# Modulation halves in another order and at other places, key and query projections interleaved by halves

## The reference

```python
def adaln_params(cond, w_mod, b_mod):
    m = jax.nn.silu(cond) @ w_mod + b_mod          # w_mod[i]: 1024 x 6144
    return jnp.split(m, N_MOD, axis=-1)            # six components of 1024

# layer 0: attention; layer 1: pooling; then both the same:
hx = modulate(x, sh1, sc1)                         # h * (1 + scale) + shift
x = layer_norm(ALPHA * x + g1 * y_lat, ln_g[i, 0], ln_b[i, 0])
x = layer_norm(ALPHA * x + g2 * swiglu(modulate(x, sh2, sc2), ffn_w_in[i], ffn_w_out[i]),
               ln_g[i, 1], ln_b[i, 1])
```

## Time and profile before

| | us |
|---|---|
| three runs, median (lowest, highest) | 1374.47 (1372.9, 1379.59) |
| the profiled execution, its own time | 1374.82 |
| its span in the trace | 1373.0 |
| TensorE busy | 1189.5 (87%) |
| VectorE busy | 819.4 (60%) |
| ScalarE busy | 489.8 (36%) |
| mean granted clock of TensorE, share of full speed | 0.932 |

### The profile page before, as it was taken

How to read it: one execution, slowest core, us unless ns; L and a number is a source line. 1 busy time by engine, 2 the same in 40 slices (tenths; PEclk the granted TensorE clock), 3 DMA queues, 4 the chain that set the end, 5 groups by cost and what they waited for, 6 DMA issues and landing times.

```text
span 1373.0 us, 17100 instructions
## 1 busy us (share of the span) xinstructions
PE 1189.5 (87%) x7007; PEld 1011.6 (74%) x7007; DVE 819.4 (60%) x1163; ACT 489.8 (36%) x676; POOL 92.3 (7%) x33
## 2 busy tenths in 40 slices
PE   3899997777777897799999699949999898899998
PEld 1676865677666876699997588847877646799977
DVE  3557476476666766776555665677865425555543
ACT  3224334232222232333433344523444433433332
POOL 0000100000000000000000002321224200000000
PEclk9899998989889999899999899978899999999999
DMA  9991531728666668259555346601012244455553
GB/s 347 327 323 62 214 117 51 283 72 288 219 225 230 249 230 291 77 177 303 185 188 176 116 157 214 184 32 62 32 62 92 65 145 137 132 184 178 183 185 111
DMA packets 145663, 236.97 MB, mean 173 GB/s; under 512 B 4918, under 2 KB 86323, under 8 KB 145459
## 3 DMA queue, kind: packets, MB, share of 16 engines
q1 hardware_dynamic: 138656, 221.12, 47.5%
q10 hardware_dynamic: 6930, 14.77, 3.3%
HBM read 229.32 MB, written 6.55 MB: 172 GB/s over the span
## 4 chain that ended last, share of the span: by engine, by line
PE 62%; DVE 13%; issue 9%; DMA 7%; ACT 5%; POOL 2%; SPq 1%; ACTq 1%; POOLq 0%; DVEq 0%
PE bank L525 59%; DMA ring<-in_ffn_w_in 7%; DVE ring_lo L1360 4%; ACT w_hi L1029 3%; DVE modacc L1481 3%; PE bank L567 3%; POOL small L2133 1%; SPq L2188 1%; POOL ring_lo L2124 1%; DVE small L2008 1%; DVE y_tok L1669 1%; DVE small L1672 1%; ACT hc_hi L1078 0%; ACTq L1061 0%; DVE y_tok L1666 0%
## 5 line engine op out<-in xcount | busy, mean ns | idle before, releaser
L1360 DVE TENSOR_TENSOR ring_lo<-ring,w_hi 128x2048 fp32r<-128x2048 f32 (+4 forms) x142 | 314.3, 2214 | 328.6 <-ACT w_hi L1029 328.6
L1029 ACT ACTIVATE w_hi<-ring 128x2048 fp32r<-128x2048 f32 (+4 forms) x154 | 285.8, 1858 | 517.6 <-PE bank L525 410.4
L525 PE MATMUL bank<-h_hi,w_hi 128*128 128x256 f32 x1056 | 303.8, 288 | 3.7 <-DVE h_lo L1379 2.1
L525 PE MATMUL bank<-h_lo,w_hi 128*128 128x256 f32 x1056 | 299.6, 284 | 0.0
L525 PE MATMUL bank<-h_hi,ring_lo 128*128 128x256 f32 x1056 | 299.3, 283 | 0.0
L525 PEld LDWEIGHTS bank<-h_hi,w_hi 128*128 128x128 f32 x1056 | 204.0, 193 | 6.9 <-issue 6.9
L525 PEld LDWEIGHTS bank<-h_lo,w_hi 128*128 128x128 f32 x1056 | 203.7, 193 | 2.3 <-issue 2.3
L525 PEld LDWEIGHTS bank<-h_hi,ring_lo 128*128 128x128 f32 x1056 | 203.5, 193 | 0.0
L525 PE MATMUL bank<-w_hi,h_hi 128*128 128x512 f32 (+4 forms) x320 | 130.5, 408 | 10.1 <-DVE h_lo L1600 4.4
L525 PE MATMUL bank<-ring_lo,h_hi 128*128 128x512 f32 (+4 forms) x320 | 126.4, 395 | 0.0
L525 PE MATMUL bank<-w_hi,h_lo 128*128 128x512 f32 (+4 forms) x320 | 125.9, 393 | 0.0
(11 more groups left out here) (223 smaller groups left out, 1598.8 us busy)
## 6 DMA issues: line engine op xcount, KB each, us to landing
aux<-in_w_mod SPq DMA_DIRECT2D x24, 2048.0 KB, 9.8
ring<-in_ffn_w_in SPq DMA_DIRECT2D x88, 512.0 KB, 5.8
ring<-in_w_in SPq DMA_DIRECT2D x24, 1024.0 KB, 4.9
ring<-in_w_ffn_in SPq DMA_DIRECT2D x44, 512.0 KB, 4.6
ring<-in_ffn_w_out SPq DMA_DIRECT2D x20, 1024.0 KB, 5.2
ring<-in_attn_w_qkv SPq DMA_DIRECT2D x12, 1024.0 KB, 13.1
ring<-in_w_ffn_out SPq DMA_DIRECT2D x10, 1024.0 KB, 5.0
bias_rows<-srow ACTq DMA_DIRECT2D x1, 5376.0 KB
```

Of the source, the lines that this page charges most:

```text
L525: return nc.tensor.matmul(o, l, r, start=start, stop=stop, **kw)
L1029: nc.scalar.activation(panel_part(i, 0), raw_panel(i), ACT.Copy).then_inc(w_hi, 1)
L1360: V.tensor_tensor(panel_part(i, 1), raw_panel(i), panel_part(i, 0).bitcast(F32), ALU.subtract)\
```

## The change

The order of the ten later components becomes 2, 3, 4, 9, 5, 6, 7, 8, 10, 11 (`COMPS`), and their products stand elsewhere: halves 0 to 7 in attention, 8 to 13 in ffn0_in (blocks 0, 2, 3, 5, 6, 8), 14 to 17 in ffn0_out, in quarters, and 18 and 19 in ffn1_in as before. `halves_before` places their loads anew. The first group's keys and queries run as K half 0, Q half 0, K half 1, Q half 1, with the second pair of first loads, the transposes of the later half of the tokens and their products on banks 6 and 7 behind Q half 0. The second group's keys begin behind the first transposed probabilities. On the output projection of attention the last loop runs tokens outside, columns inside, and VectorE makes the low parts of panels 16 and 17 behind the statistics. Both halves of the folded pooling rows are made in block 10 of ffn0.

```diff
-QKV_ORDER = (2, 0, 4, 3, 1, 5)
+QKV_ORDER = ((2, 0), (0, 0), (2, 1), (0, 1), (4, 0), (4, 1),
+             (3, 0), (3, 1), (1, 0), (1, 1), (5, 0), (5, 1))
...
+        COMPS = (2, 3, 4, 9, 5, 6, 7, 8, 10, 11)
...
-        HALF_AT = {("ffn0", nb): [6 + nb] for nb in range(10)}
-        HALF_AT.update({("ffn0_out", 0): [16], ("ffn0_out", 1): [17], ("ffn1", 1): [18], ("ffn1", 2): [19]})
-        COMP_AT = {("ffn0", 2): 5, ("ffn0", 4): 6, ("ffn0", 6): 7, ("ffn0", 8): 8, ("ffn0", 10): 9, ("ffn1", 4): 11}
+        HALF_AT = {("ffn0", 0): 8, ("ffn0", 2): 9, ("ffn0", 3): 10, ("ffn0", 5): 11, ("ffn0", 6): 12, ("ffn0", 8): 13,
+                   ("ffn1", 1): 18, ("ffn1", 2): 19}
+        COMP_AT = {("ffn0", 3): 5, ("ffn0", 6): 6, ("ffn0", 9): 7, ("ffn1", 4): 11}
...
-                if name == "ffn0":
-                    mod_sums(10)
+                    if name == "ffn0":
+                        mod_sums((8, 10)[nb])
...
+            def first_keys_and_queries():
+                wait_emptied(pe, ("pre", PK - 1))
+                for j in range(4):
+                    keys(0, 0, j)
+                queries(0, 0)
+                for n in (2, 3):
+                    mod_rows_first(n, "misc")
+                for n in (2, 3):
+                    mod_columns_first(n, "misc")
+                for ch in range(PK, KC):
+                    tokens(ch, "misc")
+                wait_emptied(pe, ("pre", KC - 1))
+                for j in range(4):
+                    keys(0, 1, j)
+                queries(0, 1)
+                swap_keys(0)
+                swap_keys(1)
+            def second_keys_and_queries():
+                turn_probs(0)
+                for i in range(8):
+                    if i:
+                        values(i - 1)
+                        turn_probs(i)
+                    keys(1, i // 4, i % 4)
+                    if i == 3:
+                        mod_sums(3)
+                values(7)
+                queries(1, 0)
+                mod_sums(4)
+                swap_keys(2)
+                swap_keys(3)
+                queries(1, 1)
...
-            for nb in range(2):
-                for tt in range(TT):
+            for tt in range(TT):
+                for nb in range(2):
                     wo(nb, 1, tt)
@@ ACT @@
-            split_to(2)
-            for h in range(4):
+            split_to(3)
+            for h in range(3):
                 key_copy(h)
             split_to(4)
+            key_copy(3)
...
             split_to(8)
-            probs_copy(3)
+            squares(0)
             key_copy(4)
-            squares(0)
             probs_copy(4)
             key_copy(5)
             probs_copy(5)
@@ DVE, maxima_and_mixes @@
+                    if 3 <= u <= 6:
+                        mod_product((2, 7)[hg], [u - 3])
@@ DVE @@
+            split_to(2)
             mod_product(0)
-            split_to(2)
+            split_to(3)
             mod_product(1)
-            split_to(3)
+            split_to(4)
             turn_pair("K", 0)
-            split_to(4)
             turn_pair("K", 1)
+            turn_pair("Q", 0)
             split_to(5)
-            turn_pair("Q", 0)
             turn_pair("Q", 1)
             mod_finish(2)
             maxima_and_mixes(0)
-            mod_product(2)
+            mod_product(3)
+            mod_finish(3)
+            mod_product(4)
             split_to(8)
-            mod_product(3)
             head_var(0)
             head_norm(0)
+            mod_product(5)
             split_to(9)
             head_var(1)
             split_to(10)
             head_norm(1)
-            mod_finish(3)
+            mod_finish(4)
             turn_pair("K", 2)
             turn_pair("K", 3)
-            mod_product(4)
             split_to(11)
+            mod_product(6)
             turn_pair("Q", 2)
             turn_pair("Q", 3)
             maxima_and_mixes(1)
             o_lows(0)
-            mod_product(5)
@@ DVE, residual_stats @@
-                    split_to(last + (2 if nb == 0 and stage != "poolw" else 1))
+                    split_to(last + (0 if stage == "wo" else 2 if nb == 0 and stage != "poolw" else 1))
...
             def out_products(nb):
-                split_to(panel_at[("ffn0_out", nb, 1)] + 2)
-                for m in HALF_AT[("ffn0_out", nb)]:
-                    mod_product(m)
+                for i in range(4):
+                    split_to(panel_at[("ffn0_out", nb, 1 + i)] + 2)
+                    if nb == 1 and i == 0:
+                        mod_finish(8)
+                        ...
+                    mod_product(14 + 2 * nb + i // 2, range(2 * (i % 2), 2 * (i % 2) + 2))
@@ SP @@
-            halves_before = {RING: [0, 1], 6: [2], 7: [3], 11: [4], 12: [5], 15: [6], 17: [7]}
-            for m in range(8, N_HALVES):
-                halves_before[{16: 40, 17: 43, 18: 50, 19: 52}.get(m, 2 * m + 6)] = [m]
+            halves_before = {RING: [0], 5: [1], 6: [2], 7: [3], 10: [4, 5], 11: [6], 12: [7], 15: [8], 17: [9], 24: [10],
+                             28: [11], 30: [12], 34: [13], 38: [14], 39: [15], 43: [16], 46: [17], 49: [18], 51: [19]}
```

More of the change, by code:

```diff
@@ L140, in ffn @@
                 add((name + "_out", nb, kg), w_out, kg, min(PK, FC - kg * PK), nb * NB, nb * NB + NB)
-    for nb in QKV_ORDER:
-        for kg in range(2):
-            add(("qkv", nb, kg), a["attn_w_qkv"][0], kg, PK, nb * NB, nb * NB + NB)
+    for nb, kg in QKV_ORDER:
+        add(("qkv", nb, kg), a["attn_w_qkv"][0], kg, PK, nb * NB, nb * NB + NB)
     for kg in range(2):
@@ L415, in build @@
         FIRST = (0, 2, 1, 3)
-        N_FIRST, N_HALVES = 4, 20
+        COMPS = (2, 3, 4, 9, 5, 6, 7, 8, 10, 11)
+        N_FIRST, N_HALVES = 4, 2 * len(COMPS)
+        turn_of = {comp: i for i, comp in enumerate(COMPS)}
         def mod_first_panel(eng, n):
@@ L685, in queries @@
                     if kg == 0:
-                        take(("Q", 2 * hg + pr), "dense")
+                        take(("Q", 2 * hg + pr), "out" if hg == 0 else "dense")
                     bank = psum[where[("Q", 2 * hg + pr)][0]]
@@ L777, in values_and_scores @@
                     scores(8 * hg + u)
[L780 to L803, removed]
+            first_keys_and_queries()
             values_and_scores(0)
-            keys_and_queries(1, first_heads)
+            second_keys_and_queries()
             values_and_scores(1)
@@ L817, in wo @@
                 if tt == 0:
-                    held["o"] = panel(("wo", nb, kg))
+                    held["o", nb] = panel(("wo", nb, kg))
                 if kg == 0:
@@ L822, in wo @@
                 for c in range(PK):
-                    ins = product(bank, token_tile(hT, kg * PK + c, tt), [x[:, c, :] for x in held["o"]],
+                    ins = product(bank, token_tile(hT, kg * PK + c, tt), [x[:, c, :] for x in held["o", nb]],
                                   kg == 0 and c == 0, kg == 1 and c == PK - 1)
@@ L844, in _ @@
             wo(1, 0, 0)
-            mod_sums(4)
+            mod_sums(9)
             wo(1, 0, 1)
@@ L1155, in _ @@
             scores_out(0)
-            for u in range(3):
+            for u in range(4):
                 probs_copy(u)
             split_to(8)
-            probs_copy(3)
+            squares(0)
             key_copy(4)
-            squares(0)
             probs_copy(4)
@@ L1743, in ffn @@
                     split_to(panel_at[(name + "_in", nb, 0)] + 2)
-                    for m in HALF_AT.get((name, nb - 1), []):
-                        mod_product(m, range(KC // 4, KC // 2))
+                    if (name, nb - 1) in HALF_AT:
+                        mod_product(HALF_AT[(name, nb - 1)], range(KC // 4, KC // 2))
                     split_to(last_panel(name + "_in", nb) + 2)
@@ L1755, in ffn @@
                     ins = V.tensor_tensor(lo, v3(t, 2), hi.bitcast(F32), ALU.subtract)
-                    if name == "ffn0" and nb in (8, 9):
-                        step(ins)
-                        settle()
-                        ins = fold_rows(nb - 8, t)
+                    if name == "ffn0" and nb == 10:
+                        for half in range(2):
+                            step(ins)
+                            settle()
+                            ins = fold_rows(half, t)
                     empties(ins, (name, "u", nb))
@@ L1762, in ffn @@
                         mod_finish(COMP_AT[(name, nb)])
-                    for m in HALF_AT.get((name, nb), []):
-                        mod_product(m, range(KC // 4))
+                    if (name, nb) in HALF_AT:
+                        mod_product(HALF_AT[(name, nb)], range(KC // 4))
             fold_norm(4, 0)
```

52 lines of the change are left out of this document (20 added, 32 removed).

## The result

| | us |
|---|---|
| after, median of five runs (lowest, highest) | 1389.81 (1386.86, 1390.28) |
| before, beside it, five runs | 1374.89 (1372.9, 1379.59) |
| ratio | 1.0095, 95% interval 1.0070 to 1.0120 |
| profiled execution of after, its span | 1389.06, 1387.2 |
| TensorE busy, mean granted clock | 1197.2 (86%), 0.923 |

The change makes the kernel slower by 15 us. The forecast was 1371.5, in a range of 1357 to 1387.

What follows compares the result with a forecast made beforehand. It held ffn0_in bound by a loop through SyncE's queue and attention by TensorE with holes. Its terms summed to -3.0 on 1374.8, giving 1371.8, or 1371.5 as a median, with a range of 1357 to 1387 us.

Steps and rivals of the forecast that it cites:

- A: Attention's first group: later K half 1, lost cover, rotary turns and holes make it 10 us slower, bounds +4 to +13.
- B: Attention's second group: first key behind the transposed probabilities, copy waits and a second component's sums; +7.5 us, bounds +3 to +10.
- C: Second group: product 6 between panel 11's low part and the queries' turn delays the scores; +5.8 us, bounds 0 to +8.
- D: Products 2 and 7, in single steps, fit into VectorE's gaps except the last; +1.0 us.
- E: Behind `wo`: statistics start while TensorE multiplies and two low parts move behind them; -1.8 us, bounds -3.5 and -1.
- F: ffn0_in: six halves instead of ten nearly end the loop through SyncE's queue; -42.9 us, bounds -50 to -36.
- G: ffn0_out: four halves instead of two, three loads waiting in SyncE's queue; +17.4 us, bounds +9 to +22.
- halves 18 and 19: Their loads cost nothing, VectorE and SyncE reaching each before it is wanted; if late, one landing, 11 us.
- signs of being wrong: ffn0_in starting before 296, ffn0_out under 75, or ScalarE waiting for landings inside ffn0_in.
- R1: Attention's new order costs 8 us, not 22.5, as VectorE and ScalarE have room; 1357 us, chance 0.2.
- R2: ffn0_out's three blocked loads cost 4 us, most blocked panels having two others ahead in the ring; 1358 us, chance 0.15.
- R3: Late transfers behind halves in ffn0_in: three of six keep 5.2 us each; +15.6, 1387 us, chance 0.21.

Runs made afterwards that it cites:

- a_first2: The changed kernel with the first group's order, lists and banks as before and half 1's load back ahead of panel 4; 1379.07 us, ratio 1.0018.
- act_order: The changed kernel with ScalarE copying transposed probabilities 4, 5 and 6 ahead of the keys of the same number; 1385.40 us, one run.
- c_prod6: The changed kernel with VectorE multiplying half 6 ahead of the low part of panel 11 instead of behind it; 1381.18 us, one run.
- e_undone: The changed kernel with the output projection's part undone: last loop with columns outside, low parts of panels 16 and 17 ahead of the statistics; 1389.84 us, one run.
- f_sums: The changed kernel with halves 9, 11 and 13 in ffn0_in multiplied in one piece at the end of their block; 1384.03 us, ratio 1.0058.
- g_loads: The changed kernel with the loads of halves 16 to 19 moved later, ahead of panels 45, 48, 50 and 52; 1367.51 us, ratio 0.9939.
- h_load: The changed kernel with the load of half 19 ahead of panel 52 again instead of panel 51; 1381.48 us, ratio 1.0035.
- h_dve: The changed kernel, loads untouched, with VectorE making panel 51's low part behind the pooling rows instead of ahead of normalising; 1379.23 us, one run.
- b_loads: The kernel before, with only the loads of halves 8 to 15 inside ffn0_in two panels later; 1340.48 us, ratio 0.9744.
- best3: The changed kernel with repairs to both attention groups, product 6, late loads, ffn0_in's one-piece products and panel 51's low part put together; 1326.56 us, ratio 0.9645.
- e_loop: The changed kernel with only the output projection's last loop back to columns outside, low parts still behind the statistics; 1387.88 us, one run.
- best4: best3 with the output projection's last loop back to columns outside, low parts still behind the statistics; 1326.29 us, ratio 0.9643.

## Why the prediction was wrong

By its own steps, on the spans (after less before, +14.2, where -3.0 was summed up):

| step | forecast | measured | by |
|---|---|---|---|
| A, first group | +10 | +9.4 | scores, 97.48 to 106.89; a_first2, 98.49 |
| B, second group | +7.5 | +8.0 | end of Q half 0; act_order -3.6 |
| C, product 6 | +5.8 | +6.6 | 4.3 at the scores at 210.62, 2.3 in the slow work behind; c_prod6 -7.5 |
| D | +1.0 | +0.6 | first products of the later half of `wo` |
| E, statistics | -1.8 | -1.9 | hole ahead of ffn0, 11.93 to 9.98; e_undone 11.94 |
| F, ffn0_in | -42.9 | -37.2 | windows; f_sums |
| G, ffn0_out | +17.4 | +19.4 | windows, g_loads |
| halves 18 and 19 | 0 | +8.0 | h_load, h_dve |
| rest | 0 | +1.3 | not tested; from ffn1's start on all traces lie between 792 and 797 |

- **The step that failed**, 8.0 of the 17.2 us between -3.0 and +14.2, is the sentence on halves 18 and 19, "nothing, VectorE and SyncE reach each there before it is wanted". The forecast had itself worked out that product 17 ends 88.8 us into ffn0_out, and half 19 can go out only then. The diff moves that half from ahead of panel 52 to ahead of panel 51, and VectorE has panel 51's low part between the statistics and normalising. By its own numbers, 88.8 + 11 + 1.9 + 2.3 = 104 against the statistics' end near 93, this is a stall of 8 to 11 us. The forecast even had the price, "one landing, 11 us", and gave it no chance. I had followed the loads of halves 16 to 18 and stopped at the last statistics. None of its signs of being wrong came true, and those of being right nearly all did (ffn0_in from 310.6, three holes in ffn0_out): no sign looked behind that stage.
- **F** was right in kind and too large by 5.7. Its term for three sums, 9.1, came out at 13.0 (what the stage's 141.7 leave beside its 126.9 and 1.7): each wait was 1.8 where it had reckoned 1.15, and the matmuls behind it ran slow; f_sums took 6.2 of it back. The 1.7 are the slow first block, which the forecast held nowhere; it comes with the loop of part E, so that part as a whole gave 0.2 and not 1.8. SyncE's waits in the stage fell to 9.1 and no landing was waited for, as forecast.
- **G** followed the forecast within 2 us at each point: half 16 out 25.0 after the stage's start (24.7), half 17 at 44.2 (44.1), half 18 at 73.5 (71.6), the statistics at 90.9 (88.9). The half-sized panels landed 9.14 and 9.46 us after their issue, where 9.6 was taken from the earlier trace rows, the full one 10.25 for 11.0. The Trainium skill ("DMA: Bandwidth & Descriptors", Where 436 GB/s comes from) puts a core's limit at about 358 GB/s; an estimate from it is 7.3 us and a fixed cost for half and half-sized panel. The two landings of that size, 9.1 and 9.5, leave 1.8 and 2.2 for the latter, so the trace doesn't speak against it.
- **Attention** (A to E, 22.5 forecast, 22.7 measured) was right term by term, in the lowest trace of after; by the other four it would be up to 25.0. So R1 was wrong. Two slips in the working, B's terms add up to 7.2 and not 7.5, A's start of K half 1 to 71.6 and not 71.8, change nothing. R2 was wrong: the stage grew by 19.4, and 20.6 came back when the loads were moved. R3 was wrong as a mechanism, though its time, 1387, lay nearest: it blamed transfers that are late, and what was late was a load issued behind a wait.
- What the forecast did not ask is why the loads stood in ffn0_in as they did. It read the loop through SyncE's queue rightly and priced it at 5.2 per block, yet took the number of products as what had to go down. b_loads shows that the loop breaks with ten products in place.

## What to carry to other kernels

When an issuing queue works in order, a load whose buffer is not yet free holds up all behind it: place it by the time at which its buffer comes free, and try this before moving any work between stages. Whenever a diff moves such a load, follow the first panel behind it to the place in each engine's list where its parts are made, over the end of the stage too, and ask what stands behind them. A long wait in the queue is no cost by itself (best3 keeps 56.1 us of them): it costs where the transfer behind it lands too late. Undoing one part of a change can show nothing where a load's place was fitted to it; undo both together.

## What the runs showed of the hardware

- A hole's length does not say how soon TensorE is back at full clock. Behind each of these holes the transposes ahead of ffn0 begin at a granted clock of 0.50, its lower level of 1.2 GHz. Then the clock is 1.00 from ffn0's first product on in before and after's first products still have 0.50. First transposes and first products of before, then of after, and the first stretch of after at full clock:
```profile
283.02:285.02 2.00, 1.99 (x10) 1.99 (x11) 0.14 (x1) 1.27 (x3) 0.00 (x0) 0.50 0.00 0
287.92:289.92 2.00, 2.00 (x17) 2.00 (x18) 1.90 (x5) 1.42 (x4) 0.00 (x0) 1.00 0.00 0
305.68:307.68 2.00, 2.00 (x10) 2.00 (x11) 0.17 (x1) 1.29 (x3) 0.00 (x0) 0.50 0.00 0
310.58:312.58 2.00, 2.00 (x9) 2.00 (x10) 1.90 (x5) 1.38 (x4) 0.00 (x0) 0.50 0.03 8
314.58:316.58 2.00, 2.00 (x19) 2.00 (x19) 1.97 (x2) 0.00 (x0) 0.00 (x0) 1.00 0.00 0
```
  Over the first 11.6 us of ffn0_in the granted clock was 1.00 in all five kernels with columns outside in that loop (holes of 11.93 or 11.94 us in before, b_loads and e_undone, 8.61 in e_loop and best4), and 0.81 to 0.85 in all twelve with tokens outside (holes of 9.98), where the first panel took 1.7 longer. The work ahead shows no such order: 0.86 from 282.2 to 300 in after, 0.81 from 282.9 to 300 in e_loop. Why is open. The Trainium skill ("TensorE: Matmul & The Clock Gate", Loop structure matters more than you think) says that the loop nest decides whether matmuls stay warm, and its example of a bad one waits ahead of every matmul. The trace agrees that the nest matters, but here it was only the order of four groups of products ahead of one wait.
- DMA had more to give than the kernel took: ffn0_in ran at 237 GB/s in before and at 290 in b_loads, with no landing waited for.
